# A hybrid decoder trunk on one Trainium2 core: the end of the first layer's mixing, with the last two tiles in an order of their own

## The reference, cut to what matters

```
for layer in (0, 1):
    h = x + mixer(rmsnorm(x))              # layer 0: mLSTM and GLA heads, gated, @ w_out
    u = rmsnorm(h) * ffn_gain
    group   = argmax(softmax(u @ wg + bg))             # 1 of 4 groups
    experts = top2((u @ we + be) inside that group)    # 2 of 8 experts
    x = h + sum(gate_e * (silu(u @ w_gate[e]) * (u @ w_up[e])) @ w_down[e])
out = rmsnorm(x)
```

## Time and profile before

| | us |
|---|---|
| median of 3 runs | 2251.98 (2246.5 to 2251.99) |
| the profiled execution, from its first instruction to its last | 2254.6 |
| last mixer iteration ends, PE goes on with late work alone | 519.35 |
| last projection's last matmul ends | 570.88 |
| tables written | 589.6 |
| first expert's rows are turned | 598.5 |

### The profile page before, as it was taken

How to read it: one execution, slowest core, us unless ns; L and a number is a source line. 1 busy time by engine, 2 the same in 40 slices (tenths; PEclk the granted TensorE clock), 3 DMA queues, 4 the chain that set the end, 5 groups by cost and what they waited for, 6 DMA issues and landing times. The chain is left out here.

```text
span 2254.6 us, 29987 instructions
## 1 busy us (share of the span) xinstructions
PE 2116.8 (94%) x10591; PEld 1728.5 (77%) x10591; DVE 1623.2 (72%) x1963; ACT 1341.3 (59%) x1667; POOL 236.8 (11%) x253
## 2 busy tenths in 40 slices
PE   7999998998599999999998988999589999999998
PEld 5778876776488888888876877888478888888885
DVE  4561233665598888888886366776599888888886
ACT  4333324543388778787873245563177787787874
POOL 1100000000101111111102320000011111111210
PEclk9999998999799999999998988999799999999999
DMA  3112212114399999999984020002279999999996
GB/s 130 38 56 84 73 57 75 57 57 168 118 356 382 385 391 385 383 378 377 387 342 156 1 85 1 20 17 79 78 285 391 380 382 383 388 390 387 383 377 245
DMA packets 122304, 513.24 MB, mean 228 GB/s; under 512 B 27229, under 2 KB 28330, under 8 KB 87402
## 3 DMA queue, kind: packets, MB, share of 16 engines
q1 hardware_dynamic: 102490, 474.09, 55.8%
q0 software_dynamic: 18576, 33.86, 3.9%
q10 hardware_dynamic: 1152, 4.19, 0.5%
HBM read 495.03 MB, written 50.86 MB: 242 GB/s over the span
## 5 line engine op out<-in xcount | busy, mean ns | idle before, releaser
L518 DVE TENSOR_TENSOR exp_w_lo<-ring_raw,first_w_hi 128x2048 fp32r<-128x2048 f32 x192 | 438.8, 2287 | 35.3 <-ACT first_w_hi L446 35.3
L518 DVE TENSOR_TENSOR exp_w_lo<-ring_raw,exp_w_hi 128x2048 fp32r<-128x2048 f32 x192 | 438.8, 2287 | 29.7 <-ACT exp_w_hi L446 29.5
L446 ACT ACTIVATE exp_w_hi<-ring_raw 128x2048 fp32r<-128x2048 f32 x192 | 367.8, 1918 | 61.1 <-PE exp_up_out L375 33.4
L446 ACT ACTIVATE first_w_hi<-ring_raw 128x2048 fp32r<-128x2048 f32 x188 | 360.9, 1920 | 69.6 <-PE exp_up_out L375 30.4
L375 PE MATMUL exp_gate_out<-exp_w_lo,exp_x_hi 128*128 128x512 f32 x512 | 202.4, 395 | 0.0
L375 PE MATMUL exp_y_out<-exp_w_lo,exp_hid_hi 128*128 128x512 f32 x512 | 201.7, 394 | 0.0
L375 PE MATMUL exp_up_out<-exp_w_lo,exp_x_hi 128*128 128x512 f32 x512 | 199.2, 389 | 0.0
L321 POOL DMA_INDIRECT y_rows<-exp_y,base_rows_y x63 | 75.9, 1205 | 966.9 <-ACT exp_y L466 966.9
L375 PE MATMUL exp_gate_out<-first_w_hi,exp_x_hi 128*128 128x512 f32 x272 | 111.3, 409 | 7.9 <-DVE exp_x_lo L546 6.9
L375 PEld LDWEIGHTS exp_gate_out<-exp_w_lo,exp_x_hi 128*128 128x128 f32 x512 | 97.6, 191 | 19.5 <-issue 0.2
L375 PEld LDWEIGHTS exp_y_out<-exp_w_lo,exp_hid_hi 128*128 128x128 f32 x512 | 97.1, 190 | 19.1
(11 more groups left out here) (487 smaller groups left out, 4781.6 us busy)
## 6 DMA issues: line engine op xcount, KB each, us to landing
ring_raw<-in_expert_w_gate_dram SPq DMA_DIRECT2D x128, 1024.0 KB, 10.3
ring_raw<-in_expert_w_up_dram SPq DMA_DIRECT2D x128, 1024.0 KB, 10.9
ring_raw<-in_expert_w_down_dram SPq DMA_DIRECT2D x128, 1024.0 KB, 11.2
l0w_raw<-in_ab_w_in_dram SPq DMA_DIRECT2D x48, 256.0 KB, 2.8
ring_raw<-y_rows SPq DMA_DIRECT2D x8, 1024.0 KB, 4.9
finish_y<-y_rows SPq DMA_DIRECT2D x8, 1024.0 KB, 13.1
ring_raw<-in_swa_w_qkv_dram SPq DMA_DIRECT2D x5, 1024.0 KB, 9.5
base_h<-in_x_dram ACTq DMA_DIRECT2D x8, 512.0 KB, 7.0
```

Of the source, the lines that this page charges most:

```text
L446: nc.scalar.activation(split[split_slot(unit)][0][:], raw[raw_slot(unit)][:], ACT.Copy).then_inc(hi_ready, 1)
L518: nc.vector.tensor_tensor(lo[:], raw[raw_slot(unit)][:], hi[:].bitcast(F32), ALU.subtract).then_inc(lo_ready[split_slot(unit)], 1)
```

## The change

From the point at which the mixers have ended, PE, ACT and DVE no longer run the last three iterations of the shared loop. A straight sequence stands in their place, which handles a = T - 2 (tile 6) and b = T - 1 (tile 7). Before that point the order is the same on every engine.

- Banks: tiles 6 and 7 are turned into AB and C_; their sums go to G24 (6, first half), P_ (6, second), G13 (7, first) and G24 (7, second); rows from the second half of tile 5 on are turned into banks 1 and 0; the logits of tiles 6 and 7 go to P_, the last ranks to bank 0, the last entries to C_, the counts to bank 1. The waits are those of the new banks.
- The last tile's normalised rows are no longer written by DVE: ACT scales them (`scale_last_rows`) once DVE has the scale, and POOL multiplies them by the gain; then SP stores them.

```diff
+        MIXED = T - 2
+        out_bank = lambda u, half: Q_ if u < MIXED else (AB, C_)[half]
+        sum_bank = lambda u, b: P_ if u < MIXED or (u, b) == (MIXED, 1) else G13 if (u, b) == (T - 1, 0) else G24
+        row_bank = lambda u, half: Q_ if (u, half) < (MIXED - 1, 1) else bank(1 - half)
+        logits_at = lambda u: (Q_ if u < T - 2 else P_)[:, 0:36]
...
 # POOL, after its two memsets of x_rows
+                pool.wait_ge(s["last_unit_rows"], 1)
+                rows_b = chunks(slots[:, (T - 1) % SLOTS])
+                g.tensor_tensor(rows_b, rows_b, gain_row[:].rearrange("p (q k) -> p k q", k=8), ALU.mult).then_inc(s["r_rows_made"], 1)
...
 # PE: waits of project_out; turn_out and turn_rows change alike
-                        if k == 0 and 2 * u + b >= 1:
+                        if k == 0 and (u, b) == (MIXED, 0):
+                            pe.wait_ge(s["gla_copied"], T)
+                        elif k == 0 and (u, b) == (MIXED, 1):
+                            pe.wait_ge(s["h_made"], 2 * MIXED)
+                        elif k == 0 and (u, b) == (T - 1, 0):
+                            pe.wait_ge(s["s_even_made"], T)
+                        elif k == 0 and (u, b) == (T - 1, 1):
+                            pe.wait_ge(s["h_made"], 2 * MIXED + 1)
+                        elif k == 0 and 2 * u + b >= 1:
                             pe.wait_ge(s["h_made"], 2 * u + b)
...
 # PE, in place of mix(T), mix(T + 1), mix(T + 2)
+                def after_mixing():
+                    a, b = T - 2, T - 1
+                    turn_out(a, 0)
+                    turn_out(a, 1)
+                    project_out(a - 1, 1, 5, 8)
+                    project_out(a, 0, 0, 4)
+                    turn_rows(a - 1, 1)
+                    project_out(a, 0, 4, 8)
+                    route_product(a - 1)
+                    rank(a - 2)
+                    enter(a - 3)
+                    project_out(a, 1, 0, 4)
+                    turn_rows(a, 0)
+                    turn_out(b, 0)
+                    turn_out(b, 1)
+                    project_out(a, 1, 4, 8)
+                    project_out(b, 0, 0, 4)
+                    turn_rows(a, 1)
+                    rank(a - 1)
+                    enter(a - 2)
+                    project_out(b, 0, 4, 8)
+                    route_product(a)
+                    project_out(b, 1, 0, 4)
+                    turn_rows(b, 0)
+                    enter(a - 1)
+                    project_out(b, 1, 4, 8)
+                    rank(a)
+                    route_product(b, range(4))
+                    turn_rows(b, 1)
+                    route_product(b, range(4, 8))
+                    enter(a)
+                    rank(b)
+                    count()
+                    enter(b)
...
 # ACT
+                def scale_last_rows():
+                    u = T - 1
+                    act.wait_ge(s["last_scaled"], 1)
+                    a.activation(chunks(slots[:, u % SLOTS]), h[:, u].rearrange("p (q k) -> p k q", k=8), ACT.Copy, scale=scale[:, u:u + 1])\
+                        .then_inc(s["last_unit_rows"], 1)
...
+                out_high(T - 2, 0)
+                out_high(T - 2, 1)
+                scale_outputs(T - 1)
+                h_root(T - 3)
+                router_cols(T - 3, 1)
+                router_cols(T - 2, 0)
+                out_high(T - 1, 0)
+                out_high(T - 1, 1)
+                h_root(T - 2)
+                router_cols(T - 2, 1)
+                router_cols(T - 1, 0)
+                h_root(T - 1)
+                router_cols(T - 1, 1)
+                scale_last_rows()
...
 # DVE
+                factors(b)
+                out_low(a, 0)
+                residual(a - 1, 1)
+                out_low(a, 1)
+                scale_of(a - 1)
+                normed_rows(a - 1)
+                residual(a, 0)
+                gate_rows_of(b)
+                take_logits(a - 1, a - 2, a - 3)
+                out_low(b, 0)
+                mark(a - 2)
+                residual(a, 1)
+                out_low(b, 1)
+                scale_of(a)
+                normed_rows(a)
+                dve.wait_ge(s["ranked"], a)
+                entries_of(a - 2)
+                ranks_of(a - 1)
+                mark(a - 1)
+                residual(b, 0)
+                take_logits(a, -1, -1)
+                residual(b, 1)
+                dve.wait_ge(s["ranked"], a + 1)
+                entries_of(a - 1)
+                ranks_of(a)
+                mark(a)
+                scale_of(b)
+                take_logits(b, -1, -1)
+                entries_of(a)
+                ranks_of(b)
+                mark(b)
```

More of the change, by code:

```diff
@@ L1312, in project_out @@
                         for n, (x, w) in enumerate(((o_hi, w_hi), (o_hi, w_lo), (o_lo, w_hi))):
-                            last = mm(P_, x[:, k], w[:, k, b * BANK:(b + 1) * BANK], start=(k == 0 and n == 0), stop=(k == 7 and n == 2))
+                            last = mm(sum_bank(u, b), x[:, k], w[:, k, b * BANK:(b + 1) * BANK], start=(k == 0 and n == 0), stop=(k == 7 and n == 2))
                         if k == 7:
@@ L1371, in between @@
-                        if t == T + 2:
-                            route_product(T - 1, range(4))
+                        turn_out(u, 0)
                     elif part == 2:
-                        if here:
-                            turn_out(u, 1)
+                        turn_out(u, 1)
                     elif part == 3:
-                        if here:
-                            project_out(u, 0, 0, 2)
-                        if late:
+                        project_out(u, 0, 0, 2)
@@ L1380, in between @@
+                        if u >= 1:
                             turn_rows(u - 1, 1)
[L1381 to L1388, removed]
+                        project_out(u, 0, 2, 4)
@@ L1395, in between @@
[L1395 to L1399, removed]
+                        project_out(u, 1, 0, 2)
                     elif part == 6:
[L1401 to L1404, removed]
+                        project_out(u, 1, 2, 4)
@@ L1475, in _ @@
                         spread_r(2 * (g - 5) + 1)
-                for t in range(T + 3):
+                for t in range(T):
                     mix(t)
+                after_mixing()
             @block.scalar
@@ L1660, in out_high @@
                     act.wait_ge(s["o_turned"], 2 * u + half + 1)
-                    if half == 0 and u >= 1:
+                    if half == (u >= MIXED) and u >= 1:
                         act.wait_ge(s["o_made"], 2 * u)
-                    a.activation(o_hi[:, 4 * half:4 * half + 4], chunks(Q_), ACT.Copy).then_inc(s["o_hi_made"], 1)
+                    a.activation(o_hi[:, 4 * half:4 * half + 4], chunks(out_bank(u, half)), ACT.Copy).then_inc(s["o_hi_made"], 1)
                 def h_root(u):
@@ L1964, in residual @@
                     part = slice(b * BANK, (b + 1) * BANK)
[L1965 removed]
+                    v.tensor_tensor(h[:, u, part], sum_bank(u, b), slots[:, u % SLOTS, part], ALU.add).then_inc(s["h_made"], 1)
                 def gate_rows_of(t):
@@ L1973, in scale_of @@
                     dve.wait_ge(s["h_rooted"], u + 1)
-                    v.reciprocal(scale[:, u:u + 1], root[:, u:u + 1])
+                    last = v.reciprocal(scale[:, u:u + 1], root[:, u:u + 1])
+                    if u == T - 1:
+                        last.then_inc(s["last_scaled"], 1)
                     dve.drain()
```

192 lines of the change are left out of this document (91 added, 101 removed).

## The result

| | before | after |
|---|---|---|
| median of the runs, us | 2251.98 (2246.5 to 2252.12, 4 runs) | 2239.52 (2238.3 to 2243.51, 4 runs) |
| ratio, 95% interval | | 0.9949 (0.9934 to 0.9964) |
| span of the profiled execution, us | 2254.6 | 2237.5 |

Predicted were 2236.8 us, between 2231 and 2244, and 15.2 us saved. The median fell by 12.5 us, the span of the two traces by 17.1.

What follows compares the result with a forecast made beforehand. Before the experts, PE was held by a sum bank DVE emptied late, then a serial DVE routing chain. Savings 16.7 + 1.5, less 3.0 for POOL, make 15.2 us: 2251.98 to 2236.8 us, range 2231 to 2244.

Steps and rivals of the forecast that it cites:

- The late work: From 519.35 us to the last projection's sum, PE issues without holes: 34.7 us instead of 51.5, 16.7 us less.
- Keeping up: During PE's last projections, DVE and ACT deliver in time; nothing stalls, with margins of about 1 and 0.8 us.
- The tight place: DVE's tile 5 logits, then tile 7's first low part: ready at 536.9 us, wanted by PE at 538.0.
- the rival of waits that stay: PE still waits in places before the last sum: one hole gives 2242.3 us, two 2247.8; chance 0.20.
- The chain: Last tile's serial routing on DVE, last sum to tables: unhindered 17.2 us instead of 18.7, saving 1.5 us.
- POOL in the way: POOL's gain multiplication blocks DVE during the last tile's choice, costing 3.0 us (bounds 0 and 4).
- the next of these: In the last choice, the next short DVE instruction reading two SBUF tiles stands until POOL ends.
- The rows' chain: Last tile's rows through ACT, POOL and store end between 564.5 and 571.0 us, hidden before tables at 574.35.
- The whole: Sum over the kernel: 15.2 us saved, giving 2236.8 us against the median of the runs.

Runs made afterwards that it cites:

- the first experiment: The kernel before, run again with no edit to measure its repeat; ratio 1.000 (0.9986 to 1.0015), span 2252.2 us.

## Why the prediction was right

- **The late work.** Forecast 34.7 us from 519.35 us on and a last sum at 554.2; measured 34.8 from 519.05 on, and 553.86. The count of instructions by their issue distance carried it. In the old order two sum banks alone give 10.2 us of it, the new order with one bank gives 11.0, both together 16.2: so they share 5.0 us, and each has 5 to 6 us more of its own. How much of the new order's part belongs to its banks for turned outputs and rows was not tested.
- **Keeping up.** The tight place was forecast with the low part ready at 536.9 and wanted at 538.0 us; it was ready at 536.96 and nothing waited. The rows of tile 6 were wanted 0.65 us after they were ready (0.8 forecast). With one bank less a wait of 2 us appears there at once, and the low clock with it. So the rival of waits that stay had a mechanism that exists, though not in the changed kernel, which has under a microsecond to spare.
- **The chain.** Forecast to the tables 20.15 us from the last sum; measured 19.23. Of the 0.9 us between them 0.8 are POOL's, the next point. Choice to tables 8.5 as before, table to turn 8.8 for 8.9.
- **POOL in the way.** The term that was mis-sized: forecast 3.0 us, measured 2.24 (2.48 - 0.24). POOL takes 2.85 us, not 3.3, and starts while DVE has two short instructions left that it doesn't stop. The step's premise was also too narrow: "the next of these", an instruction with two tiles in SBUF. The one that stood is a TENSOR_SCALAR with one tile in SBUF and one value per partition.
- **The rows' chain.** ACT took 2.14 us, more than the 1.05 to 1.84 that the rows of before seemed to allow; all else was inside its bounds. POOL was done at 562.78, over 10 us before the tables. It was hidden, as said.
- **The whole.** 15.2 us forecast, 16.2 us in the traces from one place to another, 12.5 us in the first runs and 13.7 (10.6 to 16.9) with more. Of the error of 1.0 us in the traces 0.8 is POOL's term. The runs came out below 15.2 and not above it; their interval takes in 15.2 and 16.2, so they decide nothing between the two, and that the median lies 2.7 us over the forecast time is no measure of its steps. Executions vary by several us outside the change; from the first experiment on, the late work was always read by itself.

The Trainium skill (SBUF — State Buffer, Who interferes with whom) says that a DVE instruction with two SBUF inputs and a GpSimd instruction that reads SBUF keep each other out, and counts `tensor_scalar`, in its two-port modes, among those that can take the shared pair too. By that part of the rule the trace agrees: L134 stood for the whole rest of POOL's 2.85 us and ended 0.04 us after it. In which mode L134 ran, no run here shows. The Trainium skill (GPSIMD Engine Reference, Performance pitfalls for Q7 kernels) puts the stepped read at half as much again per element; the prediction's estimate from it, 3.6 us, is above the measured 2.85, and the measurement decides.

## What to carry to other kernels

When a pipeline drains, the stages that have ended leave buffers: give them to the stages still at work, and check first whether one more buffer in the old order already gives most of it, as here 10 of 16 us by the traces. A short instruction moved to GpSimd off the critical path can still stand in the way of VectorE on it; look for a wait of VectorE's own of the same length. Compare such a change from a place inside the trace that both kernels have, since whole runs here vary by as much as the change is worth.

## What the runs showed of the hardware that was not expected

- One POOL TENSOR_TENSOR on 128x1024 stopped a TENSOR_SCALAR on 128x32 with one SBUF tile, 2.48 for 0.24 us, in two traces of the changed kernel and in that of the one-bank kernel; without POOL's instruction it took 0.24.
- After a wait of PE of 2.06 us, matmuls went over from 0.40 to 0.63 us a microsecond later, and stayed there to 544.16 (one bank). After waits of 1.41 us (two banks, old order) they kept their length. The late work of before, with two waits of 3.07 us, had 0.87 of the clock.
- ACT's copy of 128x1024 that reads with a step of eight elements took 2.14 us, its plain pass over as many elements 1.05. POOL's with one stepped input took 2.85, the plain one 2.40.
- In the second layer the time at the low clock differs between kernels whose code there is the same: 75 us before, 75 in the changed kernel, 85 without POOL's multiplication, 65 with one sum bank (10 us windows, from the experts' first turn plus 580 us to plus 1060). From the experts' first turn to the end these four traces take 1656.1, 1655.6, 1657.2 and 1650.5 us, so the whole moves by some us either way. Why the time at the low clock differs was not tested.
